# The MoE stage of a dense block: expert outputs added to the residual rows pair by pair, in place of a gated sum behind the experts

## The reference, cut to what matters

```
g_gate = softmax(g_logits)[g_idx]                    # one of 4 groups
top_v, top_i = top_k(e_in_group, 2)                  # two of its 8 experts
gates = softmax(top_v) * g_gate
expert_block(xb, e) = (silu(xb @ w1[e]) * (xb @ w3[e])) @ w2[e]     # 1024 -> 512 -> 1024
out[t] = gates[t,0] * y[t,0] + gates[t,1] * y[t,1]   # hier_moe
x = layer_norm(ALPHA * x + f, ln_g[layer, 1], ln_b[layer, 1])       # f is out
```

## Time and profile before

| | us |
|---|---|
| median of 3 runs | 2912.27 (2910.88 to 2912.61) |
| the profiled execution, its own time | 2910.9 |
| its span, from the first to the last record | 2909.1 |
| PE busy | 2833.2 (97%) |
| DVE busy | 2168.9 (75%) |
| ACT busy | 1501.4 (52%) |
| POOL busy | 461.3 (16%) |

### The profile page before, as it was taken

One profiled execution on the slowest core, in us unless ns is written; L12 is line 12 of the kernel. 1 busy time (PEld: TensorE's weight loads), 2 busy tenths in 40 slices (PEclk: granted clock), 3 DMA queues, 4 the chain that ended last, 5 costly groups with the idle time before them and its releaser, 6 DMA issues.

```text
span 2909.1 us, 42454 instructions
## 1 busy us (share of the span) xinstructions
PE 2833.2 (97%) x16328; PEld 2472.4 (85%) x16328; DVE 2168.9 (75%) x2928; ACT 1501.4 (52%) x2002; POOL 461.3 (16%) x482
## 2 busy tenths in 40 slices
PE   9997999999959999999999999999999999999999
PEld 6686888888849999888889999899998888899998
DVE  6637999999978767666568776887776665687775
ACT  6834788888845444433235444454443332354443
POOL 3211011111011111111113111121111111131111
PEclk9998999999979999999999999999999999999999
DMA  5153999999946564332325646365643323265561
GB/s 221 44 181 111 363 382 382 382 388 389 387 140 174 146 180 131 104 104 94 103 94 146 182 143 182 97 167 156 171 133 104 102 94 103 95 158 168 155 172 58
DMA packets 169295, 515.27 MB, mean 177 GB/s; under 512 B 21504, under 2 KB 22016, under 8 KB 168832
## 3 DMA queue, kind: packets, MB, share of 16 engines
q1 hardware_dynamic: 129600, 422.38, 40.4%
q0 software_dynamic: 36992, 77.62, 12.5%
q10 hardware_dynamic: 2496, 12.48, 1.1%
HBM read 508.20 MB, written 12.58 MB: 179 GB/s over the span
## 4 chain that ended last, share of the span: by engine, by line
PE 85%; DVE 5%; issue 4%; DMA 2%; ACT 2%; POOL 1%; SPq 0%; DVEq 0%; ACTq 0%; POOLq 0%
PE bank L614 28%; PE bank L612 28%; PE bank L613 28%; DVE w_lo L1764 1%; PE bank L618 1%; ACT w_hi L1133 1%; DMA sums<-in_w_a 0%; DVE ft L2149 0%; DMA raw<-in_rec_in 0%; POOL mv L1583 0%; POOL w_lo L1548 0%; DVE st L1854 0%; PE bank L675 0%; DMA sums<-in_w_b 0%; DVE xT L2199 0%
## 5 line engine op out<-in xcount | busy, mean ns | idle before, releaser
L1764 DVE TENSOR_TENSOR w_lo<-raw,w_hi 128x1024 fp32r<-128x1024 f32 (+3 forms) x481 | 593.0, 1252 | 276.8 <-ACT w_hi L1133 270.8
L1133 ACT ACTIVATE w_hi<-raw 128x1024 fp32r<-128x1024 f32 (+1 forms) x491 | 507.6, 1046 | 291.7 <-PE bank L614 272.3
L612 PE MATMUL bank<-xf_hi,w_lo 128*128 128x256 f32 x2112 | 587.9, 278 | 8.5 <-DVE w_lo L1764 6.7
L614 PE MATMUL bank<-xf_hi,w_hi 128*128 128x256 f32 x2112 | 584.9, 277 | 0.0
L613 PE MATMUL bank<-xf_lo,w_hi 128*128 128x256 f32 x2112 | 584.7, 277 | 0.0
L612 PEld LDWEIGHTS bank<-xf_hi,w_lo 128*128 128x128 f32 x2112 | 397.1, 188 | 12.9 <-issue 10.0
L613 PEld LDWEIGHTS bank<-xf_lo,w_hi 128*128 128x128 f32 x2112 | 397.2, 188 | 2.4 <-issue 1.0
L614 PEld LDWEIGHTS bank<-xf_hi,w_hi 128*128 128x128 f32 x2112 | 397.1, 188 | 0.0
L614 PE MATMUL bank<-g_hi,w_hi 128*128 128x512 f32 x832 | 327.6, 394 | 0.0
L613 PE MATMUL bank<-g_lo,w_hi 128*128 128x512 f32 x832 | 325.9, 392 | 0.0
L1764 DVE TENSOR_TENSOR w_lo<-raw_more,w_hi 128x1024 fp32r<-128x1024 f32 x249 | 295.2, 1220 | 40.8 <-ACT w_hi L1133 36.4
(11 more groups left out here) (357 smaller groups left out, 5238.4 us busy)
## 6 DMA issues: line engine op xcount, KB each, us to landing
raw_more<-in_moe SPq DMA_DIRECT2D x249, 512.0 KB, 6.8
raw<-in_moe SPq DMA_DIRECT2D x135, 512.0 KB, 6.8
raw<-in_w_a SPq DMA_DIRECT2D x77, 512.0 KB, 6.6
raw<-in_w_b SPq DMA_DIRECT2D x76, 512.0 KB, 6.4
raw<-in_w_in SPq DMA_DIRECT2D x73, 512.0 KB, 3.7
sums<-in_w_a POOLq DMA_DIRECT2D x88, 256.0 KB, 4.5
sums<-in_w_b POOLq DMA_DIRECT2D x88, 256.0 KB, 4.4
raw<-in_w_a SPq DMA_DIRECT2D x68, 256.0 KB, 5.8
```

What stands on the lines that cost most here:

```text
L612: e.matmul(out, a_lo, b_hi, start=start, stop=False, skip_group_check=partial)
L614: return e.matmul(out, a_hi, b_hi, start=False, stop=stop, skip_group_check=partial)
L1133: e.activation(split_of(k)[0], source_of(k), ACT.Copy).then_inc(s["hi"], 1)
L1764: e.tensor_tensor(lo, source_of(k), hi.bitcast(F32), ALU.subtract).then_inc(s["lo"], 1)
```

## The change

- `ys_dram` with its 1024 slots is gone. There is `r_dram`, 512 rows, one for each token. POOL first stores the scaled residual rows (`ALPHA * x`) there (four stores, L1641 of the changed kernel).
- For each half i of a pair (i = 2n + h; `ADDED` = 32 of them) POOL gathers the residual rows of that expert's tokens (`rows_in(i)`) into one buffer `rows_r`, DVE makes `rows_r + gate * output` in place, straight out of PSUM, both halves of the width, and POOL scatters them back (`rows_out(i)`). As a token may be in both, `rows_in(i + 1)` is issued only when `rows_out(i)` has landed. Each of these transfers has 128 row numbers of which 64 at least are skipped (`hidx`, a column for each half).
- ACT copies no more expert outputs.
- The gates must lie row by row of a pair: `gate_parts` (DVE, once, behind `up(0, 0)`) makes three bf16 parts of them and the two index tables, `gate_table` (eight matmuls of PE, three small operations of DVE, once, ahead of `h_turn(0)`) sorts them.
- The router table needs three small operations fewer ahead of `gather(0)`.
- Behind the experts ACT waits for the last scatter itself and issues four loads of finished rows instead of eight; no sum is made there. `weight_sums(0, 0)` waits for the end of the experts' matmuls alone.

```diff
@@ bank_table @@
+        if n == 0:
+            use("gates", "lgc", 5, (turn[0] + 2) % RING)
@@ scalar_program, down(n, h) @@
-                e.wait_ge(s["dnm"], 2 * n + h + 1)
-                if h == 0 and n >= 3:
-                    e.wait_ge(s_scatter[n % 3], scattered(n % 3, n))
-                e.activation(ye[rows, n % 3, 0:T], bank_of(("dn", n, h, 0))[rows, :], ACT.Copy).then_inc(s["yea"], 1)
@@ scalar_program, behind the experts @@
-            e.wait_ge(s["rows"], TT + 2)
-            for n in range(2 * TT):
-                tt, k = n // 2, n % 2
-                e.dma_start(ysl[:, n, :], ys_dram[k * T + tt * P:k * T + (tt + 1) * P, :]).then_inc(s_y[tt], 16)
+            e.wait_ge(s["rsum"], 16 * ADDED)
+            e.wait_ge(s["rst"], 16 * TT)
+            e.wait_ge(s["x1d"], 16 * TT)
+            for tt in range(TT):
+                e.dma_start(x_tok[:, tt, :], r_dram[tt * P:(tt + 1) * P, :]).then_inc(s_y[tt], 16)
@@ pool_program @@
+            def rows_in(i):
+
+                e.indirect_dma_start(
+                    rows_r[:, :], None, r_dram, bass.IndirectOffsetOnAxis(ap=hidx[:, i % 2, i // 2:i // 2 + 1], axis=0),
+                    bounds_check=T - 1, oob_is_err=False).then_inc(s["rin"], 16)
+
+            def rows_out(i):
+                e.wait_ge(s["yea"], i + 1)
+                e.wait_ge(s["yev"], i + 1)
+                e.indirect_dma_start(
+                    r_dram, bass.IndirectOffsetOnAxis(ap=hidx[:, i % 2, i // 2:i // 2 + 1], axis=0), rows_r[:, :], None,
+                    bounds_check=T - 1, oob_is_err=False).then_inc(s["rsum"], 16)
...
-            for n in range(NPAIR + 1):
-                if n + 2 < NPAIR:
-                    gather(n + 2)
-                if n >= 1:
-                    e.wait_ge(s["yea"], 2 * n)
-                    e.wait_ge(s["yev"], 2 * n)
-                    e.indirect_dma_start(
-                        ys_dram, bass.IndirectOffsetOnAxis(ap=sidx[:, n - 1:n], axis=0), ye[:, (n - 1) % 3, :], None,
-                        bounds_check=2 * T - 1, oob_is_err=False).then_inc(s_scatter[(n - 1) % 3], 16)
+            for tt in range(TT):
+                e.wait_ge(s["rows"], tt + 3)
+                e.dma_start(r_dram[tt * P:(tt + 1) * P, :], x_tok[:, tt, :]).then_inc(s["rst"], 16)
+            gather(2)
+            e.wait_ge(s["rst"], 16 * TT)
+            e.wait_ge(s["idx"], 4)
+            rows_in(0)
...
+            for i in range(ADDED):
+                if i % 2 == 0 and i // 2 + 3 < NPAIR:
+                    gather(i // 2 + 3)
+                rows_out(i)
+                e.wait_ge(s["rsum"], 16 * (i + 1))
+                if i + 1 < ADDED:
+                    rows_in(i + 1)
@@ vector_program, down(n, h) @@
+                e.wait_ge(s["dnm"], 2 * n + h + 1)
+                e.wait_ge(s["rin"], 16 * (2 * n + h + 1))
+                e.scalar_tensor_tensor(rows_r[rows, 0:T], bank_of(("dn", n, h, 0))[rows, :], gtab[rows, n:n + 1],
+                                       rows_r[rows, 0:T], ALU.mult, ALU.add).then_inc(s["yea"], 1)
                 e.wait_ge(s["used"], at["moe2", 2 * n + h, FET - 1] + 1)
-                e.tensor_copy(ye[rows, n % 3, T:D], bank_of(("dn", n, h, 1))[rows, :]).then_inc(s["yev"], 1)
+                e.scalar_tensor_tensor(rows_r[rows, T:D], bank_of(("dn", n, h, 1))[rows, :], gtab[rows, n:n + 1],
+                                       rows_r[rows, T:D], ALU.mult, ALU.add).then_inc(s["yev"], 1)
@@ vector_program, behind the experts @@
-                    e.wait_ge(s_y[tt], 32)
-                    e.scalar_tensor_tensor(x, y1, gate1, x, ALU.mult, ALU.add).then_inc(s["sum"], 1)
-                    e.scalar_tensor_tensor(x, y2, gate2, x, ALU.mult, ALU.add).then_inc(s["sum"], 1)
+                    e.wait_ge(s_y[tt], 16)
                     statistics(tt, 4 * TT)
```

More of the change, by code:

```diff
@@ L312 @@
 cvv dnm ehi elo fin fin_a fin_g fin_p fo fta ftd fu ga gat gex ghi gl glo gm gr gs hd hh hhi hi hlo htn idx ix
-lgc lgm lo lo_pool mm mvp out par pp pr pu pz res ri rkm rout router rows rs1 rs2 rs3 rt1 rtc sc1 sd sg sil sl
+lgc lgm lo lo_pool mm mvp out par pp pr pu pz res ri rkm rin rout rst rsum router rows rs1 rs2 rs3 rt1 rtc sd sg sil sl
 smm snap spa spp spr sq sqr srec stm stt sum tbm th tmc tmf tmm tsm turn un used uu vv wsum wt x1d x1g x1t xgf
@@ L329, in build @@
         s_sum = [ctx.enter_context(nc.semaphore(f"s_sum{i}")) for i in range(4)]
-        s_scatter = [ctx.enter_context(nc.semaphore(f"s_scatter{i}")) for i in range(3)]
         bank = [ctx.enter_context(nc.psum_tensor(f"bank{i}", [P, 512], F32)) for i in range(8)]
@@ L757, in down, with gate_table @@
                     f.then_inc(s["used"], 1)
+            def gate_table():
+                b = free_bank("gates")
+                e.wait_ge(s["idx"], 4)
+                for n in range(2 * TT):
+                    f = e.matmul(b[:, 0:3 * NBLK], oneh[:, n, :], numg[:, n, :, :].rearrange("p q n -> p (q n)"),
+                                 start=n == 0, stop=n == 2 * TT - 1)
+                f.then_inc(s["tbm"], 1)
             spin(16)
@@ L766, in tensor_program @@
                         down(n - 1, h)
+                if n == 0:
+                    gate_table()
                 if n < NPAIR:
@@ L1650, in pool_program @@
                     e.indirect_dma_start(
[L1651 to L1652 removed]
+                        r_dram, bass.IndirectOffsetOnAxis(ap=gidx[:, NPAIR + x:NPAIR + x + 1], axis=0), rows_r[:, :], None,
+                        bounds_check=T - 1, oob_is_err=False).then_inc(s["b_store"], 16)
                 e.wait_ge(s["b_store"], 16 * EXTRA)
[L1655 to L1663 removed]
             def squares(p, first, last):
@@ L1688, in weight_sums @@
                     e.dma_start(up_raw(i, j, m, 1)[:, 0:T], high[m][:, 0:T], accum_op=ALU.add).then_inc(s_sum[2 + m], 16)
-            e.wait_ge(s["sum"], 4 * TT - 1)
+            e.wait_ge(s["used"], C_DENSE)
             weight_sums(0, 0)
@@ L2040, in up, with gate_parts, gate_table @@
                     .then_inc(s["hd"], 1)
+            def gate_parts():
+                gates = sm[:, 11:13, :].rearrange("p k a -> p (k a)")
+                e.wait_ge(s["gat"], 3)
+                step(e.tensor_copy(gpart[:, 0, :], gates))
+                step(e.tensor_tensor(grest[:, 0, :], gates, gpart[:, 0, :], ALU.subtract))
+                step(e.tensor_copy(gpart[:, 1, :], grest[:, 0, :]))
+                step(e.tensor_tensor(grest[:, 1, :], grest[:, 0, :], gpart[:, 1, :], ALU.subtract))
+                step(e.tensor_copy(gpart[:, 2, :], grest[:, 1, :]))
+                step(e.tensor_scalar(other[:, 0:1], consts[:, C_ROW4:C_ROW4 + 1], 4.0 * FIRST - 2.0, float(8 * T),
+                                     ALU.is_gt, ALU.mult))
+                step(e.tensor_scalar(other[:, 1:2], other[:, 0:1], -1.0, float(8 * T), ALU.mult, ALU.add))
+                for h in range(2):
+                    step(e.tensor_scalar(Tb(1), Tb(2), other[:, h:h + 1], None, ALU.add))
+                    step(e.tensor_copy(hidx[:, h, :], Tb(1)[:, 0:NPAIR]))
+                for q in range(3):
+                    f = e.tensor_tensor(numg[:, :, q, :], blkh[:, :, :],
+                                        gpart[:, q, :].unsqueeze(2).to_broadcast([P, 2 * TT, NBLK]), ALU.mult)
+                f.then_inc(s["idx"], 1)
+            def gate_table():
+                b = bank_of("gates")
+                e.wait_ge(s["tbm"], 2)
+                step(e.tensor_copy(gtab[:, :], b[:, 2 * NBLK:3 * NBLK]))
+                step(e.tensor_tensor(gtab[:, :], gtab[:, :], b[:, NBLK:2 * NBLK], ALU.add))
+                e.tensor_tensor(gtab[:, :], gtab[:, :], b[:, 0:NBLK], ALU.add).then_inc(s["lgc"], 1)
+                e.wait_ge(s["lgc"], 5)
             def h_turn(n):
@@ L2060, in vector_program @@
                         up(n, h)
+                    if n == 0 and h == 0:
+                        gate_parts()
                     if n >= 1:
                         down(n - 1, h)
+                if n == 0:
+                    gate_table()
                 if n < NPAIR:
@@ L2070, in vector_program @@
                 e.wait_ge(s["yea"], 2 * NPAIR)
-                for i in range(3):
-                    e.wait_ge(s_scatter[i], scattered(i, NPAIR))
                 for x in range(EXTRA):
@@ L2094, in vector_program @@
                     e.wait_ge(s["b_pe"], 15 * x + 15)
-                    if x >= 1:
-                        e.wait_ge(s["b_store"], 16 * x)
-                    e.tensor_copy(ye[:, 0, 0:T], bank[5][:, :]).then_inc(s["b_dve"], 1)
-                    e.tensor_copy(ye[:, 0, T:D], bank[6][:, :]).then_inc(s["b_dve"], 1)
+                    e.wait_ge(s["rin"], 16 * (ADDED + x + 1))
+                    for half in range(2):
+                        o = slice(half * T, (half + 1) * T)
+                        e.scalar_tensor_tensor(rows_r[:, o], bank[5 + half][:, :], gtab[:, NPAIR + x:NPAIR + x + 1],
```

(1 more changed line is left out.)

60 lines of the change are left out of this document (17 added, 43 removed).

## The result

The changed kernel takes 2995.25 us (median of 4 runs, 2982.27 to 3001.05), the kernel before 2912.44 in the same session (2910.88 to 2913.24): 1.0277 times as long, interval 1.0259 to 1.0295. The profiled execution took 3001.05. The forecast was 2916, in a range of 2900 to 2948.

The account below looks back on a forecast made before the run. The prediction took PE's matmuls to bound the experts (34.04 us a pair), with a chain of waits behind them. From 2910.9 us it took 10.6 off, added 1.7 and 13.7, giving 2915.7, say 2916; range 2900 to 2948.

Parts of the forecast that it names:

- The rows of half a pair: In the experts: scatter-then-gather chain exceeds its 15.65 us by 0.44 us, paid 31 times; loss 13.7 us.
- the landing of 7.15 us: In the experts: time from issue to landing assumed for each half-pair scatter and gather among weight loads.
- Rival 2: In the experts: landings do not shrink with the rows; 2937 us, or 2978; the longer case, from 2930, got 25%.
- chain of 16.1 us: Between two halves' additions: POOL reaction 0.87, scatter 7.15, reaction 0.87, gather 7.15, and 0.05 us.
- Behind the experts: After the last scatter: four loads instead of eight, last statistics begin near 841.1 not 851.64; gain 10.6 us, bounds 8.5 and 12.6.
- the form of the loss: In the experts: DVE's addition waits for the rows_r DMA, about 0.5 us each; PE under 100%, a pair 34.9 us.
- Rival 1: In the experts: landings under 6.9 us make the chain cost nothing; 2902 to 2907 us; hidden case 30%.
- rival 3: In the experts: DVE becomes the bound by itself, 33.7 of 34.04 us; 2907 us; no chance of its own given.
- the cover of 1.70 us: DVE's spare time in a pair: two more additions take 1.36 us of it; loss 0 to 0.3 us each, taken as nothing.
- Start: Before and at the first experts: gate_parts 1.7 and gate_table 0.6 us lost, 0.6 gained; net loss 1.7 us.
- the 0.6 to be gained: At the start: three small operations fewer ahead of the first gather, 0.65 us, taken as 0.6.
- More bytes cost next to nothing: In the experts: 64 more rows a pair, 2% more bytes, cost nothing as such; at most 11 us of transfer time.

Follow-up runs that it names:

- e9: e2 with one link put back: the gather for half 0 waits for half 1's scatter of the pair before; 2925.31 us, 1.0045 times the kernel before.
- e2: Changed kernel with experts reordered so neighbours share no token, two row buffers, gather waiting only for the scatter before the last; 2911.56 us, 0.9999 of the kernel before.
- e3: Changed kernel with all row numbers of half 0 beyond the bound, so its gather and scatter move nothing; 2989.73 us, one run.
- e5: Changed kernel with a POOL memset of 128 x 300 ahead of half 0's scatter; 3004.41 us, 1.0312 times the kernel before.
- e8: Changed kernel with reordered experts, no row gathers or DVE additions, one accumulating scatter for each pair; 2908.81 us, 0.9983 of the kernel before.
- e10: e8, but the last pair has its rows gathered a pair ahead, added on DVE and scattered plainly; 2902.70 us, 0.9969 of the kernel before.
- e6: Changed kernel with three DVE copies (64 x 512, out of PSUM) added behind half 0's additions; 2968.33 us, 1.0188 times the kernel before.
- e7: Kernel before the change with a POOL memset of 128 x 620 ahead of each pair's scatter; 2914.06 us, 1.0003 times the kernel before.
- e12: Changed kernel with reordered experts and the same row numbers, those of both experts, for both halves' gathers and scatters; 3012.71 us, one run.
- e13: Changed kernel with all row numbers of half 1 beyond the bound; 2986.16 us, one run.
- e1: Changed kernel with one DVE copy (64 x 512, out of PSUM) added behind half 0's additions; 2969.04 us, 1.0201 times the kernel before.

## Why the prediction was wrong

**Failed: "The rows of half a pair", the landing of 7.15 us that was taken "for both".** The sentence before it took the scatter of before, 7.5 us with an issue of 1.87, as what a scatter in the midst of the weight loads takes. It was what a scatter takes at that one place, behind `hT_lo`. The changed kernel has a second place, behind half 0's additions, where the splits stand back to back, and there the issue takes 4.56 and the landing 10.67. With measured landings that link is 0.87 + 10.67 + 0.87 + 7.29 + 0.05 = 19.8 us against 16.0 of time (17.5 from half 0's output to half 1's, less two additions of 0.75): 3.7 us of excess, 16 times 60. Measured from the end of one output to the end of the next, these 16 steps take 60.6 us more than before. Rival 2 had named the fact ("takes 1.87 us for it beside a busy DVE, 0.98 beside an idle one"), and stopped there, with one price for "busy", where the same busy DVE gives 1.87 at one place and 4.56 at another.

**A reading that was wrong and did no harm.** The prediction gave both links half a pair, 17.02 us. In the earlier trace rows the halves are 17.5 and 16.5. Its own chain of 16.1 us would then fit the long half and lose 0.9 us on the short one, 15 times 14 us: the same sum, by luck. (Behind the experts 851.64 less 841.1 is 10.5, not 10.6.)

**Left out: what follows a stall.** By the same terms the other link is 0.87 + 6.23 + 0.87 + 7.53 + 0.05 = 15.55 us against 15.0 of time (16.5 less 1.5), 8 us in 15 steps; its additions wait 2.8 us in all. Yet those 15 steps take 30.8 us more than before. The prediction had no term for PE's clock, and the trace has one: of the 92.1 us between the first output and the last, PE is idle for 64.0, as long as the additions wait, and 28.1 are the same matmuls at a lower granted clock (0.94 in the mean). How much of the 30.8 is the clock and how much DVE making splits again before PE has work, no run separates. The last addition ends 96.2 us later than the last copy did, 4.1 of that from the start.

**Right: the form of the loss.** A row of waits of DVE's addition for the DMA of `rows_r`, PE under 100%, and landings from which the sign follows. With one link alone (e9) the landings were 7.06 and 7.22, and the excess 0.78 against the 0.44 of the forecast. Rival 1 (the chain hides) and rival 3 (DVE the bound) needed e2 to come about. There rival 3's price, up to 0.3 us a pair, measured 0.34: the cover of 1.70 us was used up, as 4 additions of 0.745 us take 1.60 more than 2 copies of 0.69; at 682 ns each it would have been 1.36.

**Right: behind the experts, size short.** Gain 13.6 us where 10.6 was forecast and 12.6 was the bound. The transfers of the weight sums, half of which were put ahead of the fourth load (2 us), came behind all loads, and the last scatter landed in 2.7 us, not 5.1 (from 826.32 to the loads at 831.46 in the earlier trace rows).

**Start: loss, size short.** 3.1 us behind the experts' first split, where 1.7 + 0.6 = 2.3 was forecast; the 0.6 to be gained lies ahead of it, where the traces of kernels with the same program differ by 2 us and show nothing so small. Split by split on DVE, the changed kernel was 1.0 us later than before at the experts' first one (272.6 us of before) and 4.1 later at the one of 304.0, behind `gate_table`; in e2, e3, e5 and e9 the growth between these two is 3.1 to 3.2 as well. At `gate_parts` alone the delay grows by 3.3 us, so little of its steps was hidden. With three steps fewer, and nothing else waiting for them, e8 and e10 lost 0.9.

**More bytes cost next to nothing: right.** 23.07 MB are written instead of 12.58, and e2, which has them all, takes 0.34 us a pair more. The 15.20 MB of e8, which reads no rows and adds none on DVE, cost nothing (34.04). Whether the 0.34 are DVE's additions, which use up what it had to spare, or in part the bytes, no run separates.

**The rule that the prediction weighed.** The Trainium skill, "DMA: Bandwidth & Descriptors", section "Anatomy of one DMA — SWDGE (gpsimd) path", gives some 2.3 us for such a transfer. In the experts it is further off in this kernel than in the one before: 6.2 to 10.7. Behind them, with hardly a load about, the last scatter landed in 2.7.

**What the skill says of the issue.** The Trainium skill, "SBUF — State Buffer", section "Who interferes with whom", has GpSimd and a DVE operation with two SBUF inputs exclude each other while GpSimd reads SBUF, the later one blocked until the other ends; a DVE operation with at most one SBUF input, outside DVE's two-port modes, does not. The trace agrees in part: an issue ends 0.85 to 0.91 us after the end of a split, and takes 1.18 us beside copies out of PSUM (e6). But it can be held over several splits, which a wait for the one that runs does not give. The page also infers that making a transfer's packets is not held up by such an operation. For these transfers, which follow a table of row numbers, the runs show that it is.

**Open** is why POOL gets in at the end of the first split at half 1's place, in all traces, and at half 0's mostly at that of the third or fourth. The point within a split (e5, e7) and the list (e3, e12, e13) don't decide it. Nor does the length of the row of splits: four follow without a pause at both places (551.10 and 574.20 above). Nor does the token gather that POOL issues ahead of half 0's scatter: the last three of the changed kernel have none, and take 4.57, 4.56 and 3.43. In the changed kernel every issue that lasts to the fourth split ends where DVE pauses, for 0.28 us, and no scatter's issue in any trace lasts beyond a pause of DVE; those that end sooner need no pause. Open is also why half 0's landing is longer by 1.7 us more than its issue (10.67 - 6.23 = 4.44 against 2.69).

## What to carry to other kernels

A transfer that POOL issues has a price for its place. Before a chain is built on one, look at what DVE runs behind the point of issue; a duration read at one place need not hold at another. A chain of transfers that must fit into a fixed time should not be costed at a margin of 0.4 us when one of its terms was measured at one place; free it first (other order, second buffer, gather ahead, or let the transfer add by itself), then the same work cost 0.3 us a pair (e2) or nothing (e8).

## What the runs showed of the hardware that was not expected

- POOL's issue of one and the same scatter of 128 row numbers took from 1.0 to 5.8 us, by what DVE ran beside it, and 1.2 to 4.6 at one and the same place (e9). Where it was held up, it ended 0.85 to 0.91 us after the end of a split.
- Work added to DVE, on which PE waited, made the kernel faster (e1, 26 us; e6, 27 us), and a transfer without a single row took as long to issue as a full one (e3). The changed kernel's stalls cost PE twice: 64.0 us of idle time and 28.1 us of slower matmuls behind it.
- An accumulating scatter of 128 rows took 6.4 us to land behind the experts, a plain one 2.7 to 5.0 (2.7 for half a pair, 3.7 and 5.0 for a whole one, in e10 and before); in the experts its issue took 2.48 us (the row gives least, median and most in ns) at the place where a plain one takes 1.87.

```profile
L1636 POOL DMA_INDIRECT r_rows<-ye,sidx x15: 2453/2476/2495, 338.2 to 813.6; - x15
```
